# The last exponential of each unit ahead of the unit's reading, the convolution's tap and the next high weights

## What is computed

```python
h = rms_norm(x, norm_g)
proj = jnp.einsum('bsd,de->bse', h, w_in) + b_in
...
y_a = indexer_sparse_attention(a_q, a_k, a_v, i_q, i_k, i_w)     # 8 heads, 128 best keys of each row
y_b = chunked_relpos_attention(b_q, b_k, b_v, rel_bias)          # 8 heads, 9 chunks of 64 keys
qk = jax.nn.silu(causal_depthwise_conv(jnp.concatenate([c_q, c_k], axis=-1), conv_w, conv_b))
y_c = mlstm_chunkwise(c_q, c_k, c_v, c_i, c_f + f_bias, c_o)     # 4 heads
...
merged = jnp.sum(gate * y, axis=2)
return x + jnp.einsum('bsd,de->bse', merged, w_out)
```

## Time and profile before

| | us |
|---|---|
| median of 3 runs | 1283.41 (1283.41 to 1283.66) |
| the profiled execution, own time | 1283.52 |
| its span in the trace | 1281.3 |
| PE busy | 1263.1 (99%) |
| DVE busy | 689.0 (54%) |
| ACT busy | 633.3 (49%) |
| POOL busy | 599.5 (47%) |

### The profile page before, as it was taken

How to read it: one execution, slowest core, us unless ns; L and a number is a source line. 1 busy time by engine, 2 the same in 40 slices (tenths; PEclk the granted TensorE clock), 3 DMA queues, 4 the chain that set the end, 5 groups by cost and what they waited for, 6 DMA issues and landing times.

```text
span 1281.3 us, 19785 instructions
## 1 busy us (share of the span) xinstructions
PE 1263.1 (99%) x6486; PEld 1064.3 (83%) x6486; DVE 689.0 (54%) x1432; ACT 633.3 (49%) x1157; POOL 599.5 (47%) x759
## 2 busy tenths in 40 slices
PE   8999999999999999999999999999999999999997
PEld 6788888888988888888888888878888888888887
DVE  6799887745545221123687988785644631121144
ACT  6565676686534332333256466767754433323233
POOL 6654333423235555455775642333322455455463
PEclk9999999999999999999999999999999999999999
DMA  7223111221322323333342321122212222332331
GB/s 296 83 82 115 67 50 58 66 91 51 113 69 70 103 82 98 99 97 108 99 158 89 99 85 65 50 66 73 76 51 102 89 82 82 106 98 90 103 102 66
DMA packets 37047, 116.35 MB, mean 91 GB/s; under 512 B 4080, under 2 KB 4464, under 8 KB 36720
## 3 DMA queue, kind: packets, MB, share of 16 engines
q1 hardware_dynamic: 34672, 111.24, 26.3%
q10 hardware_dynamic: 2304, 4.20, 1.0%
HBM read 111.23 MB, written 4.19 MB: 90 GB/s over the span
## 4 chain that ended last, share of the span: by engine, by line
PE 92%; DVE 4%; ACT 2%; issue 1%; POOL 1%; DMA 0%; ACTq 0%; SPq 0%; DVEq 0%; POOLq 0%
PE acc L653 75%; PE ps_o L812 5%; PE ps_t L799 2%; PE ps_t L790 2%; PE ps_s L768 2%; PE ps_o L819 1%; PE ps_s L774 1%; DVE turn L1371 1%; DVE bk_lo_s L1351 1%; PE ps_s L757 1%; PE acc L686 1%; PE spare L750 1%; PE spare L831 1%; DVE prob L1392 0%; DMA xT<-x 0%
## 5 line engine op out<-in xcount | busy, mean ns | idle before, releaser
L604 POOL TENSOR_TENSOR w_lo<-w_raw,w_hi 128x256 fp32r<-128x256 f32 x744 | 586.0, 817 | 664.2 <-ACT w_hi L889 664.0
L653 PE MATMUL acc<-h_hi,w_hi 128*128 128x512 f32 x1120 | 447.6, 400 | 0.7 <-POOL h_lo L615 0.7
L653 PE MATMUL acc<-h_lo,w_hi 128*128 128x512 f32 x1120 | 438.8, 392 | 0.0
L653 PE MATMUL acc<-h_hi,w_lo 128*128 128x512 f32 x1120 | 292.6, 395 | 0.0
L889 ACT ACTIVATE w_hi<-w_raw 128x1024 fp32r<-128x1024 f32 (+1 forms) x210 | 202.0, 962 | 119.5 <-PE acc L653 90.8
L653 PEld LDWEIGHTS acc<-h_hi,w_hi 128*128 128x128 f32 x1120 | 210.7, 188 | 41.7 <-POOL h_lo L615 1.8
L653 PEld LDWEIGHTS acc<-h_lo,w_hi 128*128 128x128 f32 x1120 | 210.7, 188 | 39.4
L653 PEld LDWEIGHTS acc<-h_hi,w_lo 128*128 128x128 f32 x1120 | 205.6, 188 | 40.4
L1513 DVE SCALAR_TENSOR_TENSOR gated<-prob,acc 128x512 f32<-128x512 f32 x16 | 11.0, 688 | 246.7 <-PE acc L653 246.7
L1131 ACT ACTIVATE prob<-acc,par_half 128x512 f32<-128x512 f32 x48 | 33.1, 690 | 147.1 <-PE acc L653 147.1
L1078 ACT ACTIVATE prob<-prob,neg_max 128x128 f32<-128x128 f32 (+3 forms) x128 | 70.7, 553 | 9.2 <-DVE neg_max L1392 8.9
(11 more groups left out here) (274 smaller groups left out, 1823.0 us busy)
## 6 DMA issues: line engine op xcount, KB each, us to landing
w_raw<-w_full SPq DMA_DIRECT2D x162, 512.0 KB, 3.4
w_raw<-w_mix SPq DMA_DIRECT2D x48, 256.0 KB, 2.6
rel<-rel ACTq DMA_DIRECT2D x16, 256.0 KB, 2.9
xT<-x SPq DMA_DIRECT2D x4, 512.0 KB, 6.2
stage<-x_tok SPq DMA_DIRECT2D x4, 512.0 KB, 10.1
xT<-x SPq DMA_DIRECT2D x1, 2048.0 KB, 9.3
x_kept<-xT SPq DMA_DIRECT2D x1, 2048.0 KB, 9.0
xT<-x_kept SPq DMA_DIRECT2D x1, 2048.0 KB, 8.3
```

What stands on the lines that cost most here:

```text
L604: last = pool.tensor_tensor(w_lo[:, slot, part, :], w_raw[:, raw, part, :], w_hi[:, slot, part, :].bitcast(F32), ALU.subtract)
L653: last = pe.matmul(acc[slot][:, :], w[:, slot, k, :], x[:, k, :], start=(place == 0), stop=(place == 3 * nk - 1))
```

## The change

The exp of the last item pushed in each turn of the loop over units 16 to 36 is added to the list at the end of the turn, so it stands in the last group of a unit, before the steps `rows`, `conv` part 0 and `unit`, and its place in the next group is skipped. Only ACT does anything in an `exp` step. Waits, instructions and buffers are the same.

```diff
     seq = []
     flying = []
+    early = set()
 
     def push(n):
...
         for back, kind in ((1, "exp"), (2, "turn_p"), (3, "values")) if mlstm else ((2, "exp"), (3, "turn_p"), (4, "values")):
-            if len(flying) >= back and flying[-back] is not None:
+            if len(flying) >= back and flying[-back] is not None and (kind, flying[-back]) not in early:
                 seq.append((kind, flying[-back]))
...
                 if u == U_AZ + 1:
                     seq.append(("turn_c", 0))
             k += 1
+        early.add(("exp", n - 1))
+        seq.append(("exp", n - 1))
         if 0 <= rows < 6:
             seq.append(("rows", rows))
             rows += 1
```

## The result

The changed kernel takes 1285.73 us (median of 19 runs, 1285.49 to 1286.43) against 1283.41 (19 runs): +2.3 us, ratio 1.0017, 95% interval 1.0011 to 1.0024. That is inside the 0.2% that the prediction called "same" and inside its range, but at nearly four times the +0.6 us of its sum. The profiled execution's span went from 1281.3 to 1283.6 us.

The account below looks back on a forecast made before the run. PE, holding 92% of the chain that ended last, was taken as the bound. Per layer -0.18 + 0.35 + 0.13 = +0.30, twice +0.6, gives 1284.1, or 1284.0 as the runs' median; range 1282.3 to 1286.0 us.

Parts of the forecast that it names:

- same: Whole kernel: about 0.2%, 2.6 us, can't be told from no change; the summed forecast and no effect lie within, 87%.
- The three waits on the exponential win nothing: Readings of units 28, 32 and 36: PE waits for the copy instead of the exp; gain 0.
- Gain of 0.18 at unit 29: Unit 29's reading: early transposes let the values start at 235.83 instead of 236.01, with ACT's copy unmoved; gain 0.18 us.
- The stall at 228.96, nothing: PE's 0.63 us stall before item 36's values waits for DVE to free `ps_o`, not for the exp; nothing gained.
- Unit 23, 0.13: Unit 23's reading: the exp waits for `neg_max`, delaying copy and values of item 20; new stall of 0.13 us per layer.
- Unit 24, 0.35: Unit 24's reading: the exp waits for `neg_max`, delaying copy and values of item 23; new stall of 0.35 us per layer.
- Ports, zero, bounded by 0.37 once in a layer around 228 us: POOL's later splits meet other DVE work; cost or gain at most 0.37 us per layer where DVE bounds, taken as zero.
- The sum by the rule of the Trainium skill (SBUF — State Buffer, Who interferes with whom): A port meeting could cost a whole 0.82 us subtraction, 0.8 instead of 0.37 per layer: 1285.6 in place of 1284.0.
- DVE's lateness at unit 24 is taken in: DVE's multiply-add at unit 24 comes 1.2 us late; idle times of 1.74 and 2.05 us absorb it before 220 us.
- Faster: Rival: waits on the exponential go and nothing replaces them; 3.2 us off, 1280.2, or 1278.4 without any PE idle; 5%.
- No effect: Rival: estimated stalls at units 23 and 24 don't appear, only the 0.18 gain is left; -0.4, 1283.1; 20%.
- Slower: Rival: late taps at units 24 and 25 carry DVE's lateness to stalls at units 28 and 29; +3.2, 1286.6; 8%.

Follow-up runs that it names:

- the four exps alone: Only the exps of items 36, 39, 48 and 60 moved, against the kernel before: 1282.88 us, -0.4 us, ratio 0.9996.
- the cut split: All exps moved as in the change, POOL's split of unit 25 cut to its last quarter: 1284.15 us, 0.9 us over the kernel before.

## Why the prediction was right, and where its size was off

**The three waits on the exponential win nothing:** right at units 28, 32 and 36. The values went on starting 0.05 behind the copy, and moving those exps alone gave -0.4 us where the waits add up to 3.2. Of the +0.24 at item 35, 0.10 is the restart named below; for the rest, DVE's multiply-adds before `neg_max` of item 35 took 2.25 us and had taken 1.90, again under a split that came later. The delay at item 35 is there in the other two kernels with nearly all exps moved, and not with the four exps alone, where that split keeps its time.

**Gain of 0.18 at unit 29:** it didn't appear (-0.02). The transposes were early, but the copy came 1.21 us later than before where PE had come 1.06 later. DVE's `bk_lo_s` subtractions between (L1351, now L1354) took 1.59 and had taken 1.37: the split now ended at 230.18 and reached into them from 229.83 on, where it had ended before they began. That ate what there was to win. The prediction had the copy fixed and didn't look at what DVE does ahead of it.

**The stall at 228.96, nothing:** it fell by 0.28. DVE's `bq_s` subtraction and the split, before:

```profile
224.57 0.98 DVE L1345 TENSOR_TENSOR bq_s<-bq,bq_s 64x512 fp32r<-64x512 f32 x1
```

```profile
224.28 4.16 POOL L604 TENSOR_TENSOR w_lo<-w_raw,w_hi 128x256 fp32r<-128x256 f32 x4 [7.19 <-ACT w_hi L889]
```

and after:

```profile
225.92 0.69 DVE L1348 TENSOR_TENSOR bq_s<-bq,bq_s 64x512 fp32r<-64x512 f32 x1
```

```profile
225.99 4.19 POOL L607 TENSOR_TENSOR w_lo<-w_raw,w_hi 128x256 fp32r<-128x256 f32 x4 [6.78 <-ACT w_hi L892]
```

The subtraction now started just ahead of the split and no longer behind it. No run was made for this alone, but in the kernels with only the four exps moved and with all but items 21 and 24 moved it takes 0.69 and 0.68 and the stall is shorter by as much; with item 21 or item 24 alone, which leave unit 28's exp where it was, it takes 0.96 and the stall is 0.61 and 0.62.

**Unit 23, 0.13:** 0.13. **Unit 24, 0.35:** 0.36 when measured alone. To each, 0.10 has to be added: after a stall the six matmuls of the values take 0.88 us in place of 0.78, which the sum left out; 0.4 us in all for these two places, and 0.2 more at unit 29, where the wait moved from the transposes to the values (the +0.10 at item 47 in the table).

**Ports, zero, bounded by 0.37 once in a layer around 228 us:** this is the step that failed. I looked for meetings of splits with DVE's work only where DVE was the bound before, and put them at zero because as many should end as begin, which no row said. The meeting that counted was at unit 23, where DVE and ACT had room, but the change itself had put the exp's wait for `neg_max` behind that work. It cost 0.64 in the pair of multiply-adds and 0.71 at PE's stall at unit 24 (0.91 less the 0.20 with the cut split), twice: 1.4 us. Added to the sum of 0.6, with 0.4 for the restarts, this gives 2.4; the rest of the account is smaller terms of either sign, at units 24 (0.20 and not 0.35), 28 and 29.

The sum by the rule of the Trainium skill (SBUF — State Buffer, Who interferes with whom), 0.8 per layer and 1285.6 in all, was nearer to the measured 1285.73 than my zero. That it came so near is luck: it was one subtraction at one meeting around 228 us, and what cost the time were two multiply-adds at unit 23. As a mechanism it is only half confirmed: a meeting didn't cost a whole subtraction of 0.82 us for each instruction, but 0.32. The range held because its upper end had 0.3 in reserve for each stall and 0.4 for ports in each layer; it was not made for what happened, and that it was enough is luck too.

**DVE's lateness at unit 24 is taken in:** right. `neg_max` of item 30 was ready at 199.89, 1.19 us later than before, and PE's values beside it were 1.19 later too; DVE waits for PE's scores there, so nothing of its own lateness was left.

**Rivals.** Faster fell with the four exps at the stalls. No effect fell too, as both stalls appeared at their size. Slower named another place: the lateness didn't travel to units 28 and 29. What it had right is that a late step at one unit is paid at another; the road was POOL's split and not the tap.

## What to carry to other kernels

A view of waits names what came last, not what would come next: before an operation is moved ahead of a wait, see what else the waiting engine needs a moment later, and whether that would come any sooner. Here the thing to move was not the exp but the high weights in front of the copy. Done at three units, that gave 2.15 us, nearly all of it at the two units behind which DVE had room. And an engine whose output has five microseconds in hand can still cost time when it is shifted, if its work lengthens another engine's.

## What the runs showed of the hardware

DVE's multiply-add with both inputs in SBUF (128x512, fp32) takes 0.75 us and up to 1.24 while POOL subtracts 128x256 tiles in SBUF; a pair of them 1.54 with no split beside it (1.60 with a split over its first 0.27 us) and 2.23 to 2.25 with one over most of it, and cutting the split brought it back to 1.54. DVE's subtraction of 64x512 took 0.69 alone and 0.98 under a split. PE's six `values` matmuls (128x64) take 0.88 us behind a stall where 0.78 is usual.
